# One program instead of two for the projections, the gated-linear-attention heads and the neighbourhood attention

## The reference

```python
x = layer_norm(x, ln_in_g, ln_in_b)
proj = x @ w_in                      # gq gk gv gg glr | nq nk nv
o_gla = gla_mixer(...)               # 4 heads, both directions, chunks of 64 tokens, gated
o_na = neighbourhood_attention(...)  # 8 heads, window of 8 rows x 16 columns of a 64-wide grid, bias table
mix = concat([o_gla, o_na]) @ w_out
x = layer_norm(ALPHA * x + mix, ln1_g, ln1_b)
f = conv_gated_mlp(x)                # 1024 -> 5632, conv of width 3, silu gate, -> 1024
x = layer_norm(ALPHA * x + f, ln2_g, ln2_b)
```

## Time and profile before

| | us |
|---|---|
| median of 3 runs | 3387.92 (3386.04 to 3389.48) |
| the profiled execution | 3386.37 |
| its span, first to last instruction | 3384.1 |
| last dense step of project_gla ends | 714.5 |
| first job of natten begins | 847.5 |
| last output of natten on DVE | 1274.5 to 1275.1 |

### The profile page before, as it was taken

The page is one execution under the profiler, slowest core; times in us unless marked ns, Lnnn a source line. Parts: engine busy times, 40 slices in busy tenths (PEclk is TensorE's granted clock), DMA queues, the critical chain, the costliest instruction groups (busy, mean ns, idle before and its releaser), DMA issues.

```text
span 3384.1 us, 42316 instructions
## 1 busy us (share of the span) xinstructions
PE 3177.5 (94%) x15664; PEld 2548.7 (75%) x15664; DVE 1744.9 (52%) x3389; ACT 1105.5 (33%) x2118; POOL 372.8 (11%) x374
## 2 busy tenths in 40 slices
PE   6998998885999995999999999999999999999997
PEld 4776766664777774788888888888888888888885
DVE  6647646742666663555645335353353533543377
ACT  2346245421443441444333222132222222222222
POOL 0012100004333400000003000030000200020000
PEclk9999999987999998899999999999999999999998
DMA  7799697848777738788787556575565755656553
GB/s 265 298 301 277 232 289 243 285 150 240 252 227 254 252 141 324 282 308 290 254 317 288 199 188 235 198 287 197 190 234 197 289 195 193 233 202 236 193 197 114
DMA packets 267883, 807.95 MB, mean 239 GB/s; under 512 B 44706, under 2 KB 111138, under 8 KB 220320
## 3 DMA queue, kind: packets, MB, share of 16 engines
q1 hardware_dynamic: 234784, 608.11, 52.6%
q10 hardware_dynamic: 21312, 155.20, 12.8%
q0 software_dynamic: 11584, 41.95, 3.3%
HBM read 622.04 MB, written 187.24 MB: 239 GB/s over the span
## 4 chain that ended last, share of the span: by engine, by line
PE 58%; DVE 2%; DMA 2%; ACT 0%; issue 0%; SPq 0%; POOL 0%; DVEq 0%; ACTq 0%
PE trunk_ps_h L76 12%; PE trunk_ps_h L77 12%; PE trunk_ps_h L78 12%; PE trunk_ps_f L76 7%; PE trunk_ps_f L78 7%; PE trunk_ps_f L77 7%; DMA trunk_raw<-in_w_out 1%; DMA trunk_raw<-in_w_down 1%; PE trunk_ps_h L2016 0%; DVE trunk_w L1758 0%; DVE trunk_y L1777 0%; DVE trunk_stats L1781 0%; ACT trunk_w L1675 0%; DVE trunk_y L1814 0%; DVE trunk_y L1816 0%
## 5 line engine op out<-in xcount | busy, mean ns | idle before, releaser
L76 PE MATMUL trunk_ps_h<-trunk_xt,trunk_w 128*128 128x512 f32 x1760 | 685.7, 390 | 1.4 <-DVE trunk_xt L1822 1.4
L77 PE MATMUL trunk_ps_h<-trunk_xt,trunk_w 128*128 128x512 f32 x1760 | 685.4, 389 | 0.0
L78 PE MATMUL trunk_ps_h<-trunk_xt,trunk_w 128*128 128x512 f32 x1760 | 685.4, 389 | 0.0
L1852 DVE SCALAR_TENSOR_TENSOR trunk_tt<-trunk_hb,trunk_cw,trunk_tt 128x512 f32<-128x512 f32 x220 | 187.0, 850 | 678.2 <-ACT trunk_tt L1701 678.2
L76 PE MATMUL trunk_ps_f<-trunk_w,trunk_m 128*128 128x512 f32 x1168 | 456.9, 391 | 20.6 <-DMA trunk_m<-mix_lo 19.3
L78 PE MATMUL trunk_ps_f<-trunk_w,trunk_m 128*128 128x512 f32 x1168 | 455.1, 390 | 0.0
L77 PE MATMUL trunk_ps_f<-trunk_w,trunk_m 128*128 128x512 f32 x1168 | 455.0, 390 | 0.0
L1699 ACT ACTIVATE trunk_hb<-trunk_ps_h 128x512 f32<-128x512 f32 x220 | 131.7, 599 | 885.9 <-PE trunk_ps_h L78 885.9
L76 PEld LDWEIGHTS trunk_ps_h<-trunk_xt,trunk_w 128*128 128x128 f32 x1760 | 330.9, 188 | 70.7 <-DVE trunk_xt L1822 1.8
L78 PEld LDWEIGHTS trunk_ps_h<-trunk_xt,trunk_w 128*128 128x128 f32 x1760 | 330.8, 188 | 68.9
L77 PEld LDWEIGHTS trunk_ps_h<-trunk_xt,trunk_w 128*128 128x128 f32 x1760 | 330.9, 188 | 68.5
(11 more groups left out here) (204 smaller groups left out, 4472.5 us busy)
## 6 DMA issues: line engine op xcount, KB each, us to landing
trunk_w<-wu_s SPq DMA_DIRECT2D x88, 1024.0 KB, 4.8
trunk_w<-wu_s ACTq DMA_DIRECT2D x88, 1024.0 KB, 4.8
near_xr<-xt_s SPq DMA_DIRECT2D x160, 512.0 KB, 5.8
front_xr<-xt_s SPq DMA_DIRECT2D x120, 512.0 KB, 6.3
wu_s<-trunk_w SPq DMA_DIRECT2D x44, 1024.0 KB, 4.8
trunk_w<-wd_s SPq DMA_DIRECT2D x44, 1024.0 KB, 4.8
trunk_w<-wd_s ACTq DMA_DIRECT2D x44, 1024.0 KB, 4.8
trunk_raw<-in_w_up SPq DMA_DIRECT2D x44, 512.0 KB, 5.8
```

The lines of the kernel that those rows point to most:

```text
L76: pe.matmul(out, lh, rh, start=first, stop=False, skip_group_check=skip)
L77: pe.matmul(out, lh, rl, start=False, stop=False, skip_group_check=skip)
L78: return pe.matmul(out, ll, rh, start=False, stop=last, skip_group_check=skip)
L1852: dve.scalar_tensor_tensor(out, hb[:, i, s, a_j:a_j + BLK], tap[:, a_j:a_j + 1], out, ALU.mult, ALU.add).then_inc(conv_step, 1)
```

## The change

`project_gla` and `natten` become one program, `attention`, of 320 dense steps and a tail. Steps 0 to 159 are those of before, steps 160 to 319 the pair passes. The buffers of the gated heads and those of the neighbourhood attention lie over one another, with waits for the last use of the old ones. The jobs' banks are the four of the gated heads and the fourth of `acc`. In numbers:

- Followers at step 160 or later are spread out: step 160 + d becomes 160 + 2d + 1. The outputs' scores that stood at 160, 163, 166, 169, 172 stand at 161, 167, 173, 179, 185, their products at 165, 171, 177, 183, 189, between dense steps of a pair pass.
- `JOBS_AT`: the jobs of the first pair begin at step 194 and go on at 1.5 steps (194, 195, 197, 198, ...), those of the second at 225 likewise, those of the third at 258 and of the fourth at 298 with every second step. Seen from step 160 that is 34, 65, 98 and 138, where it was 18, 58, 98 and 138.
- The ring of slices has six places filled five ahead for the pair passes too (eight and six before); that of the weights has eight (ten, and twelve in natten), and the weights are split two steps later than before. The values of a pair lie in the unused half of the weight ring and a rest buffer.
- So a pair's values come in six groups of 16 DMAs, for the first pair too: at SP's steps 176, 178, ..., 186. For the other pairs two of the groups wait for the same job and are issued together.
- The bias rows are spread to `rpb_rep` in the VG23 pass (before: in the NV pass), and those of the first pair are loaded at step 156, with the masks.
- The barrier and the second start (first slices, first weights) are gone.

```diff
+V_SLOTS = KC
+GROUPS_AFTER = ((2, 3, 4), (3, 5, 8), (5, 7, 12), (7, V_SLOTS, 16), (V_SLOTS, NKG, 16), (0, 2, 20))
+JOBS = NU * NQB
+JOBS_AT = [194 + 3 * i // 2 for i in range(JOBS)] + [225 + 3 * i // 2 for i in range(JOBS)] \
+    + [258 + 2 * i for i in range(JOBS)] + [298 + 2 * i for i in range(JOBS)]
...
-XRING, WRING, RAWS, TILES = 6, 10, 3, 8
+XRING, WRING, RAWS, TILES = 6, KC, 3, 8
...
     def shifted(steps, by):
-        return [s + by for s in steps]
+
+        return [s + by if s + by < NSTEP else NSTEP + 2 * (s + by - NSTEP) + 1 for s in steps]
...
+        ps_s, ps_t, ps_no = (bank[:, 0, :], bank[:, 1, :]), (bank[:, 2, :], acc[:, 3, :]), bank[:, 3, :]
...
-            return (p - 1) * PER_PASS + PER_PASS - KC - 1 + kc if p else kc - TURN_AHEAD
+            return p * PER_PASS - KC + 1 + kc if p else kc - TURN_AHEAD
...
+            def load_nv(p, i):
+
+                g0, g1, after = GROUPS_AFTER[i]
+                if p:
+                    sp.wait_ge(pv_done, (p - 1) * JOBS + after)
+                else:
+                    sp.wait_ge(stepped, NSTEP)
+                    for u in range(UNITS):
+                        sp.wait_ge(out_stored[u], 16 * stored_by(NPASS * NBLK))
+                by_row = tok_nv[:, p * P:(p + 1) * P].rearrange("(g a c) d -> a c g d", a=KG, c=GRID_W)
+                for cb in range(NQB):
+                    for a in range(KG):
+                        sp.dma_start(nv(g0, g1, cb)[a * BAND:(a + 1) * BAND],
+                                     by_row[a, BAND_AT[cb]:BAND_AT[cb] + BAND, g0:g1]).then_inc(nv_in[i], 16)
...
-            for u in range(UNITS):
-                sp.wait_ge(out_stored[u], 16 * stored_by(NPASS * NBLK))
-            sp.wait_ge(rep_done, 32 * ROWS_U)
+                if n == NSTEP - 4:
+                    load_masks()
+                    load_bias(0)
+                for i, (_, _, after) in enumerate(GROUPS_AFTER):
+                    if n == JOBS_AT[0] - 18 + 2 * i:
+                        load_nv(0, i)
+                    for p in range(1, PAIRS):
+                        if n == JOBS_AT[(p - 1) * JOBS + after - 1] + 9:
+                            load_nv(p, i)
+                for p in range(1, PAIRS):
+                    if n == JOBS_AT[p * JOBS] - 30:
+                        load_bias(p)
+                for j in job_at(n, 10):
+                    if jobs[j][2] == NQB - 1:
+                        store_no(j)
+            for i in range(2):
...
+            def make_tables(p):
+                pool.wait_ge(bias_in, (p + 1) * 16 * ROWS_U)
+                if p == 0:
+                    pool.wait_ge(masks_in, 32)
+                    pool.wait_ge(z_done, NIN)
+                    pool.wait_ge(cum_done, 2 * NIN)
+                    pool.wait_ge(q_in_done, NIN)
+                    pool.wait_ge(k_end_done, NIN)
+                    pool.wait_ge(u_done, 2 * NIN)
...
+
+            def evict_pair(n):
+                B, b = n // KC - NPASS * NBLK, slice_of(n)[0]
+                order = "p (b a c) -> p a b c"
+                dve.wait_ge(nqk_hi, 2 * B + 1)
+                dve.tensor_tensor(nq[:, 1, b, :].rearrange(order, b=NQB, c=QB_C),
+                                  acc[:, (2 * B) % 3, :].rearrange("p (a b c) -> p a b c", b=NQB, c=QB_C),
+                                  nq[:, 0, b, :].bitcast(F32).rearrange(order, b=NQB, c=QB_C), ALU.subtract).then_inc(nqk_lo, 1)
+                dve.wait_ge(nqk_hi, 2 * B + 2)
+                dve.tensor_tensor(nk[:, 1, b * BLK:(b + 1) * BLK], acc[:, (2 * B + 1) % 3, :],
+                                  nk[:, 0, b * BLK:(b + 1) * BLK].bitcast(F32), ALU.subtract).then_inc(nqk_lo, 1)
```

More of the change, by code:

```diff
@@ L505, in _ @@
                     scale_keys(i)
+                if n == NSTEP + 1:
+                    for p in range(PAIRS):
+                        make_tables(p)
         @block.scalar
@@ L651, in _ @@
                     squares(j)
+                if NSTEP <= n < DENSE and n % KC == KC - 1:
+                    evict_pair(n)
+                for j in job_at(n, 8):
+                    if jobs[j][2] == NQB - 1:
+                        no_out_hi(j)
+                for j in job_at(n, 6):
+                    copy_turned(j)
+                for j in job_at(n, 2):
+                    exps(j)
         @block.vector
@@ new lines, in turn_weights @@
+            def turn_weights(j):
+                groups = UNITS_NA[jobs[j][1]][1]
+                if j == 0:
+                    pe.wait_ge(normed, NOUT)
+                    pe.wait_ge(copied[UNITS - 1], NPASS * NBLK)
+                for side in range(2):
+                    pe.wait_ge(p_done, 2 * j + side + 1)
+                    need(pe, pt_dve if side else pt_act, j)
+                    for g in range(groups):
+                        mm = pe.transpose(ps_t[side][:, g * P:(g + 1) * P], s[:, j % N_S, side, g * P:(g + 1) * P], ident[:])
+                    mm.then_inc(t_done, 1)
@@ new lines, in weigh_values @@
+            def weigh_values(j):
+                p, u, cb = jobs[j]
+                first, groups, _, _ = UNITS_NA[u]
+                if j == 0:
+                    pe.wait_ge(o_lo, NOUT)
+                pe.wait_ge(pt_act, j + 1)
+                pe.wait_ge(pt_dve, j + 1)
+                if cb == 0:
+                    need(pe, no_lo, unit_no(j))
+                    for i, (g0, g1, _) in enumerate(GROUPS_AFTER):
+                        if g0 < first + groups and first < g1:
+                            pe.wait_ge(nv_in[i], 16 * NQB * KG * (p + 1))
+                for g in range(first, first + groups):
+                    for side in range(2):
+                        mm = pe.matmul(ps_no[half_of(side), cb * P:(cb + 1) * P], nv(g, g + 1, cb)[:, 0, half_of(side)],
+                                       pt[:, j % 2, side, (g - first) * P:(g - first + 1) * P], start=g == first,
+                                       stop=g == first + groups - 1)
+                mm.then_inc(pv_done, 1)
```

673 lines of the change are left out of this document (285 added, 388 removed).

## The result

The changed kernel takes 3454.68 us (median of 4 runs, 3449.71 to 3457.35), the kernel before 3386.98: a ratio of 1.0198, 95% interval 1.018 to 1.0215. The direction was right, the size was not: 68 us slower where 22 were forecast. That is above the forecast's own range of 3394 to 3428 us, and 15 us above the 3440 to which the wider range reached.

A forecast was written before the change was run, and what follows sets the result against it. TensorE, busy 94% of the span, was taken as the bound. 3386.4 - 74.3 (join's idle time and half clock) + 15 + 30 + 4 + 22.5 + 5.8 + 6 + 13.3 gave 3409 us, 0.65% slower; range 3394 to 3428, chance 0.46.

The forecast's parts named there:

- Late slices: Join, steps 160 to 193: TensorE waits for slices loaded too late, 15 us until step 173 and 30 us after.
- SP's hold for an output: Join: SP, held until an output is normalised, issues slices late; 15 us until step 173, then 3.0 and 3.0.
- the value groups: Join: five groups of value DMAs, 8.0 us each on SP, make slices late by 24.0 us of the 30.
- 34 dense steps: Join, steps 160 to 193: 34 dense steps at 1.4 us, with 32.0 us of other work 79.6 us.
- most of it is hidden, as the next slice is late anyway; I take 4 us, and 0 to 12 as bounds: Join: the lower clock after TensorE's holes mostly costs nothing extra; 4 us, bounds 0 to 12.
- rival 3: Join and jobs: the lower clock after holes is not hidden, 28 us more, 3437 us; chance 0.15.
- The term of the scores' waits: Denser jobs, steps 194 to 257: scores wait for VectorE's bias pass, 22.5 us, plus 5.8 where block copies fall in front.
- the plain chain: Denser jobs: copy, normalising and bias pass on VectorE outlast one dense step; 18 waits of 1.25 us, 22.5 us.
- Two value groups together: Jobs, SP's steps 225, 256 and 297: 32 DMAs in 16.0 us make the next slice late, 13.3 us in all.
- At nothing: Weight ring, first pair's tables, bias copies' move and later jobs priced at no cost; the bias copies -5 to +5 us.
- Rivals 1 and 2: 1: join's value groups are hidden, 3372 us, chance 0.16; 2: denser jobs cost nothing, 3375 us, chance 0.13.
- Rival 4: Gains and losses cancel: slices land at 3.1 us, chains are 20% shorter, 15 us less, 3394 us; chance 0.10.

The follow-up runs named there:

- e12: The changed kernel with the first pair's value groups issued by POOL behind its first tables, the other pairs' staying on SP: 3430.91 us, ratio 1.0132.
- e4: The changed kernel with the last five outputs' operands loaded three steps before their scores (the first's five) instead of eight: 3423.71 us, ratio 1.0106.
- e7: The changed kernel with the edits of e12, e4, e2 and e3 together: 3359.01 us, ratio 0.9921 to the kernel before.
- e13: e7 with the bias pass also ahead of a block's eviction, and masks and first bias rows loaded at SP's step 128: 3352.24 us, ratio 0.9897.
- e2: The changed kernel with the bias pass first in VectorE's step, before the copy of turned weights and the normalising: 3425.83 us, ratio 1.0111.
- e14: The changed kernel with the splitting of a pair's next weights last in a step on ScalarE and VectorE: ratio 1.0178 to the kernel before.
- e15: e7 with the bias pass also ahead of a block's eviction, and with e14's edit: 3336.46 us, ratio 0.9853 to the kernel before.
- e10: The changed kernel without POOL's tables for the second to fourth pair, all jobs using the first pair's: 3440.16 us, ratio 1.0162.
- e3: The changed kernel with the later pairs' fifth value group issued four steps behind the fourth, undoing the double group: 3443.22 us, ratio 1.0169.
- e9: The kernel before, with the 16 copies of the bias table to rpb_rep in the VG23 pass instead of the NV pass: ratio 1.0005.
- e11: The kernel before, with the weights of project_gla's second to fourth pass split two steps later: ratio 0.9975.
- e1: The changed kernel with all value loads issued by POOL between its tables instead of by SP: 3446.28 us, ratio 1.0175.

## Why the prediction missed

- **The join's plan was right, its sum in part by luck.** Late slices 45 us, 45.4 measured; e12 and e4 show both of its causes, SP's hold for an output (forecast 21 us, the waits until 789 are 26.1) and the value groups (24.0; the waits behind are 19.3). The two errors of 5 us cancel. The single slices at the holds came out otherwise as well: 7.5, 4.6, 3.0 and 3.0 us were forecast, 2.9, 9.0, 9.1 and 5.2 measured. The operand of an output that was 4.3 us late stood in no term. The count of 34 dense steps is one short, but the sum goes by idle time and doesn't use it.
- **The step that failed is "most of it is hidden, as the next slice is late anyway; I take 4 us, and 0 to 12 as bounds".** The clock cost 24.6 us in the join. In twelve of the thirteen kernels of the table it stands at 0.36 to 0.51 of the join's waits: 24.6 to 50.1, 16.5 to 35.9 (e12), 10.7 to 27.8 (e4), 2.9 to 7.0 (e7); e13, 7.0 to 4.7, is off that line. The waits did not shrink for it: those at SP's holds were 26.1 us for 21. A slower TensorE only shortens the next wait if what it waits for doesn't go through TensorE, and at SP's holds it does: SP waits for a normalising, which waits for products, which run at the lower clock. (That this is why is argued from the order, no run takes the clock away alone.) This is rival 3, with the chance of 0.15: it had 28 us more than the forecast, and 30 were measured (24.6 + 15.2 less the 10 that the forecast had).
- **The term of the scores' waits was mis-sized**, 28.3 for 44.9 us. e2 shows that its mechanism is right (30.5 us by order alone), and the waits under 2.5 us, 24.5 together, are near the 22.5 of the plain chain. What was missing: the splits of the next weights stand ahead of a bias pass in the first two pairs' jobs, behind raw weights that SP's bias rows and value groups hold (e14, e15), and POOL's tables lengthen the normalising (e10, 7.4 us of waits). I had priced the tables' work on POOL, not what it does to VectorE, and had put the weight ring at nothing.
- **Two value groups together** were sized rightly, 13.2 for 13.3, but e3 shows that the wait's size was not its worth: without it others grew.
- **At nothing**: the bias copies are at nothing (e9). The splits two steps later were worth -8 us in steps 0 to 159 (e11), as its expectation had it: a raw weight that SP waits to load has a low-rank operand behind it, and the wait for that operand fell from 6.8 to 0.5 us.
- Rivals 1 and 2 fell: slices were late by 58.6 us in all, scores waited 48.0. Rival 4, the smaller sum, fell with them.

Open stays how POOL slows VectorE, and why the clock cost more in e13 than its waits let expect.

## What to carry to other kernels

A queue that issues for several consumers turns one consumer's wait into everyone's: before two programs are joined, list what each DMA queue waits for, and give transfers that must wait a queue of their own or a later place. Put first in a step, on the helping engine, what the bounding engine waits for, ahead of evictions and splits that are due later. Price a hole of the matrix engine at up to one and a half times its length where what it waits for depends on its own work.

## What the runs showed of the hardware

In a join with holes of 1 to 9 us TensorE's lower clock cost 0.36 to 0.51 of the holes' length again, by the estimate above (24.6 us for 50.1 in the changed kernel; e13, with 7.0 for 4.7, is the exception). VectorE's short passes from SBUF to SBUF took 1.3 to 1.4 times as long in the mean while POOL had tables to make among them (554 for 418 ns, 233 for 170), and the shortest 3.4 times with POOL issuing DMAs as well (586 for 170, e1). A DMA of the value groups took 0.53 us of POOL's time (8.42 us for 16 in e12) and about as much of SP's (7.62 us for 16 at 787.65 in the changed kernel, 0.48 each).
